# A decoder layer on one core: arrays between stages kept by chunk in DRAM, and the scan stage with another order of loads, of ACT's work, of the mask and of the keys

## The chip, the core and the metric

The kernel runs on one core of a Trainium2 chip. A core has TensorE (PE in the profile), VectorE (DVE), ScalarE (ACT), GpSimd (POOL) and SyncE (SP), each with an instruction stream of its own, and 16 DMA engines that all queues share. The metric is the device time of one execution in microseconds, the median of several.

## What is computed

One inference step of a hybrid decoder layer, all in float32: 1024 prompt tokens and 8 sample tokens of width 1024. One projection feeds two head groups, a state-space scan (SSD, 16 heads of 64, state of 128, two groups) and an mLSTM (4 heads, keys and values of 256); their outputs go through a product and a layer norm, then through PEER, a layer with product keys and gathered expert rows. Both scans go over the prompt in 8 chunks of 128 tokens. The part that matters here, per chunk:

```python
# SSD scan
acs = jnp.cumsum(dtc * a, axis=1)
lmat = jnp.exp(jnp.where(mask, acs[:, :, None] - acs[:, None], -jnp.inf))
mm = cb[..., None] * lmat * dtc[:, None]
y = jnp.einsum('btsgh,bsghp->btghp', mm, xc)
y = y + jnp.einsum('btgn,bghpn->btghp', cc, h) * jnp.exp(acs)[..., None]
h_new = h * jnp.exp(acs[:, -1])[..., None, None] + jnp.einsum('bsgn,bsgh,bsghp->bghpn', bc, decay, xc)
# mLSTM scan
att = jnp.einsum('bthd,bshd->btsh', qc, kc) * jnp.exp(dmat - m_t[:, :, None])
num = jnp.einsum('btsh,bshv->bthv', att, vc) + w_inter[..., None] * jnp.einsum('bthd,bhdv->bthv', qc, c)
c_new = w_old[..., None, None] * c + jnp.einsum('bsh,bshd,bshv->bhdv', w_s, kc, vc)
```

with `q = u_c @ w_mq` and `k = (u_c @ w_mk) * DK**-0.5`. The kernel returns the outputs of the layer and the new states of the prompt and of the eight samples.

## The kernel before

Three stages follow one another, with a barrier over all engines between them (line 107).

The **first stage** (`build`, up to line 442) makes the projection. Channels, 20 tiles of 128 (`NCT`), come out with tokens along the free dimension, go through a convolution on DVE into `cv[q]` (two buffers, q = 0, 1, line 438), through Silu on ACT (L309), and are stored by ACT's queue into `cht_d` (L311), a tile at a time: 128 rows of 1032 tokens. The rows of gates (`nacs`, `mrun`, ...) go into `rows_d`, 48 rows of 1024 tokens. DVE writes `cv[q]` again once its store has landed. What is needed by token (z, v, o) goes into `tok_d`.

The **second stage**, `build_scan`, works a chunk at a time, and beside each chunk i it updates the states of sample i. Five streams are written out by hand, one for each engine, and meet by semaphores; `pairs` runs the first two chunks written out and the other six as a loop. In a chunk i:

- SP loads `rows` (48 x 128, L600), `rb` (24 of these rows, each sent to all 128 partitions, L604), `cht` (all 20 channel tiles of the chunk's 128 tokens, L606), v (L614), and, once the mix of chunk i-1 is made (`dve_mix`), z and o (L618); then the four loads of the sample's states (`st`, `bb`, `cs`, `vb`, L623 to L626). `rb` is one buffer: its load waits until chunk i-1 has read it, and `cht` until PE's product with the state (`pe_ys`) of chunk i-1.
- PE transposes `rows`, B and x from `cht` (L660 to L668), makes q and k with channels on the partitions (L677), and then k again with tokens on the partitions (L684, `two(0)`, the source of `kw`); then the product of k and q (L690), the 16 transposes of the mix of chunk i-1 (L574), y (L700), the state's part of y (L705), the new state (L709), and the mLSTM's products up to L741, with one-column products for the sums (L718, L727, L736, and L749 for the sample).
- POOL writes `L`, the logarithms of the decays: `rb` plus a mask that is 1e30 above the diagonal (L891), 20 x 128 elements a partition. After it come `dx` (L900), `xdec` (L904), `og`, the o gate (L907), and the decay of `hT` (L909), in this order.
- ACT copies PE's transposes (`cols`, `btok`, `xtok`, L804 to L806), makes the small exponents (L809 to L816), then `root` of chunk i-1 (L566 and L568: exp(-0.5 ln) of the variances in `rs`, with a table load ahead of each of the two), then the 16 exponents of `L` (L821), the copies of q and k (L825, L826), 4 more exponents (L828), and the store of the mix of chunk i-1 (`mix_store`, L583, L586).
- DVE makes `xdt`, `kw`, `L` times C B (L948), the sums for y, the norms' statistics, the new states, and in `head_out` the variances (last L551, `dve_var`); then it waits for `root` (L553) and makes the mix (L556 to L561).

After chunk 7 ACT sends four output arrays (L859 to L862), does `root` of chunk 7, and the samples' tail follows.

The **third stage**, `build_peer`, reads `mixt_d` by chunk and quarter (L1176), and takes the rest of the time.

## Time and profile before

| | |
|---|---|
| median of 3 runs | 3868.72 us (3864.3 to 3871.62) |
| the profiled execution: its time / its span | 3861.48 us / 3859.7 us |
| first stage, span | 0 to 627.0 us |
| second stage, span | 627.0 to 1130.9 us |
| third stage, span | 1130.9 to 3859.7 us |
| busy over the span: PE, DVE, ACT, POOL | 89%, 69%, 22%, 45% |
| DMA | 1083.20 MB, mean 281 GB/s |

Times in the profile are in microseconds from the start of the span. A row of the timeline is one instruction or a run of like ones; in brackets stands how long the engine had been idle before it, and what ended that. SPq and ACTq are the queues that issue DMAs; the time of such a row is that of the issue, not of the transfer. A wait is put down to the last of its causes.

### The profile page before, as it was taken

How to read it: one execution, taken by the hardware profiler on the slowest of the kernel's cores; microseconds unless marked ns; L12 is line 12 of the kernel's file. 1: busy time of each engine (PE TensorE's matmuls, PEld its weight loads, DVE VectorE, ACT ScalarE, POOL GpSimd, SP SyncE). 2: the span in 40 equal slices, each digit the busy share in tenths (PEclk: the TensorE clock that was granted, in tenths of full speed). 3: DMA queues.
4: the chain of work that ended last, by engine and by line, in shares of the span. 5: the costliest groups of instructions: out<-in, count | busy, mean ns of one | idle time of the engine just before them, and what ended most of it. 6: DMA issues, size and time to landing. Idle time of an engine off the chain costs nothing.

```text
span 3859.7 us, 46342 instructions
## 1 busy us (share of the span) xinstructions
PE 3428.5 (89%) x15419; PEld 2392.4 (62%) x15419; DVE 2653.1 (69%) x5587; ACT 838.2 (22%) x1679; POOL 1743.5 (45%) x1432
## 2 busy tenths in 40 slices
PE   7999995988868899989997766699999999999997
PEld 6999995877743344434443443477667676667764
DVE  6660000666744789988998889777777777777776
ACT  2211111454420111121112233211111111111110
POOL 2332221222201466656765345455555555555552
PEclk9999997888879999999998989799999999999998
DMA  3333324566654799989998787999999999999996
GB/s 100 99 121 112 128 96 152 160 170 180 169 198 163 274 362 355 356 330 356 368 348 294 252 296 237 343 373 394 392 372 389 386 383 376 380 398 385 389 376 215
DMA packets 442316, 1083.20 MB, mean 281 GB/s; under 512 B 49872, under 2 KB 208048, under 8 KB 438160
## 3 DMA queue, kind: packets, MB, share of 16 engines
q0 software_dynamic: 186624, 679.56, 47.2%
q1 hardware_dynamic: 182872, 304.79, 23.3%
q10 hardware_dynamic: 72632, 96.56, 7.1%
q8 instruction: 91, 1.49, 0.2%
q14 instruction: 97, 0.79, 0.1%
HBM read 987.76 MB, written 93.02 MB: 280 GB/s over the span
## 4 chain that ended last, share of the span: by engine, by line
PE 49%; DVE 9%; DMA 8%; issue 3%; ACT 1%; POOL 1%; SPq 0%; DVEq 0%; ACTq 0%; POOLq 0%
PE PB L1921 15%; PE PB L1908 12%; PE PB L1944 8%; PE PB L1884 6%; PE PB L1866 4%; DMA x1d<-in_peer_u 3%; PE PB L1897 3%; DMA vbf<-in_peer_v,gix 3%; DVE ub L1609 2%; DVE oha L1553 1%; DMA ub<-in_peer_u,gix 1%; PE PB L1988 1%; DVE ohb L1555 1%; ACT stag L1750 1%; DVE acc L1644 1%
## 5 line engine op out<-in xcount | busy, mean ns | idle before, releaser
L1346 POOL DMA_INDIRECT ub<-in_peer_u,gix x640 | 701.7, 1096 | 855.4 <-DVE hid L1609 597.2
L1346 POOL DMA_INDIRECT vbf<-in_peer_v,gix x640 | 739.0, 1155 | 365.5 <-issue 192.8
L1921 PE MATMUL PB<-vbd,wd 128*128 128x512 f32 x1536 | 684.3, 595 | 0.0
L1944 PE MATMUL PB<-vbf,dg 128*128 128x512 f32 x1020 | 523.9, 640 | 156.1 <-ACT dg L1787 120.8
L1908 PE MATMUL PB<-xds,uts 128*128 128x384 f32 x3072 | 572.0, 341 | 0.0
L1908 PEld LDWEIGHTS PB<-xds,uts 128*128 128x128 f32 x3072 | 534.2, 190 | 0.5 <-issue 0.5
L1609 DVE CUSTOM_DVE_ANT_0 ub<-ub,x1g 128x1024 f32<-128x1024 f32 x384 | 467.7, 1223 | 77.1 <-DMA ub<-in_peer_u,gix 49.2
L1921 PEld LDWEIGHTS PB<-vbd,wd 128*128 128x128 f32 x1536 | 284.0, 191 | 308.9 <-issue 308.9
L1944 PEld LDWEIGHTS PB<-vbf,dg 128*128 128x128 f32 x1020 | 194.2, 199 | 403.9 <-issue 240.2
L1569 DVE TENSOR_TENSOR uts<-PB,uts 128x512 fp32r<-128x512 f32 x256 | 175.9, 687 | 302.2 <-ACT uts L1763 302.0
L1644 DVE SCALAR_TENSOR_TENSOR acc<-vbf,wg,acc 128x1024 f32<-128x1024 f32 x257 | 329.1, 1280 | 7.0 <-DMA vbf<-in_peer_v,gix 5.8
L1609 DVE CUSTOM_DVE_ANT_0 ub<-ub,x1gb 128x1024 f32<-128x1024 f32 x256 | 311.5, 1217 | 1.5 <-DMA ub<-in_peer_u,gix 1.3
L1763 ACT CAST uts<-PB 128x512 fp32r<-128x512 f32 x256 | 149.9, 586 | 656.1 <-PE PB L1897 644.2
L1866 PE MATMUL PB<-wo,mt 128*128 128x512 f32 x576 | 271.8, 612 | 21.5 <-DMA wo<-in_w_out 16.0
L1884 PE MATMUL PB<-wp,x1T 128*128 128x512 f32 x576 | 270.9, 604 | 2.2 <-ACT x1T L1730 2.2
L269 PE MATMUL PB<-wtkh,xh 128*128 128x256 f32 (+1 forms) x864 | 244.6, 283 | 6.2 <-ACT xps L303 6.2
L269 PE MATMUL PB<-wtkh,xl 128*128 128x256 f32 (+1 forms) x864 | 243.4, 282 | 0.0
L269 PE MATMUL PB<-wtkl,xh 128*128 128x256 f32 (+1 forms) x864 | 242.7, 281 | 0.0
L915 DVE MEMSET onec<- 128x1 f32 x1 | 0.1, 59 | 343.1 <-PEq L107 343.1
L1866 PEld LDWEIGHTS PB<-wo,mt 128*128 128x128 f32 x576 | 113.0, 197 | 167.6 <-issue 150.7
L1787 ACT ACTIVATE dg<-ident,wg 128x128 f32<-128x128 f32 x255 | 100.8, 399 | 502.2 <-PE PB L1944 424.7
L1884 PEld LDWEIGHTS PB<-wp,x1T 128*128 128x128 f32 x576 | 112.2, 196 | 144.4 <-issue 141.4
(384 smaller groups left out, 5182.1 us busy)
## 6 DMA issues: line engine op xcount, KB each, us to landing
vbd<-in_peer_v SPq DMA_DIRECT2D x128, 512.0 KB, 6.9
x1d<-in_peer_u SPq DMA_DIRECT2D x96, 512.0 KB, 9.1
gd_d<-stag ACTq DMA_DIRECT2D x12, 2048.0 KB, 10.4
gbd<-gd_d SPq DMA_DIRECT2D x16, 1536.0 KB, 18.1
ubd<-in_peer_u SPq DMA_DIRECT2D x32, 512.0 KB, 9.2
wtr<-in_w_tok SPq DMA_DIRECT2D x12, 1024.0 KB, 7.5
tok_d<-stg ACTq DMA_DIRECT2D x96, 128.0 KB, 1.7
rb<-rows_d SPq DMA_DIRECT2D x8, 1536.0 KB, 27.1
```

The source lines that it names most:

```text
L269: last = nc.tensor.matmul(PB[0:n, b, 0:TW], x[:, k, t * CH:t * CH + n], w[:, k, :], start=k == 0 and v == 0, stop=k == KD - 1 and v == 2)
L1346: pool.indirect_dma_start(out=buf, out_offset=None, in_=a[table], in_offset=bass.IndirectOffsetOnAxis(ap=index, axis=0)).then_inc(done, 16)
L1569: V.tensor_tensor(uts[:, b % 2, 1, 4 * x:4 * x + 4, :].rearrange("p k e -> p (k e)"), PB[:, 7, :], uts[:, b % 2, 0, 4 * x:4 * x + 4, :].re ...
L1609: V.tensor_tensor_reduce(out=ub[:, t % NB, :], in0=ub[:, t % NB, :], in1=by, scale=1.0, scalar=0.0, op0=ALU.mult, op1=ALU.add, accum_out=i ...
L1644: V.scalar_tensor_tensor(y, vbf[:, v % NB, :], wg[:, hv % 2, kv:kv + 1], y, ALU.mult, ALU.add).then_inc(s["ax"], 1)
L1763: S.copy(uts[:, b % 2, 0, 4 * x:4 * x + 4, :].rearrange("p k e -> p (k e)"), PB[:, 7, :]).then_inc(s["utc"], 1)
L1866: last = T.matmul(PB[:, 2 + h, :], mt[:, m % 2, j % 4, :], wo[:, j, h * 512:(h + 1) * 512], start=j == 0, stop=j == 15)
L1884: last = T.matmul(PB[:, 4 + n, :].rearrange("p (h n) -> p h n", h=4), x1T[:, kk, :], wp[:, 4 * n:4 * n + 4, kk, :], start=kk == 0, stop=kk ...
L1897: last = T.transpose(PB[:, 7, j * P:(j + 1) * P], ubd[b % 4][:, (4 * x + j) * P:(4 * x + j + 1) * P], ident[:, :])
L1908: last = T.matmul(PB[:, 6, 0:TD], uts[:, b % 2, ul, k, :], xds[:, xl, k, :], start=(k, n) == (0, 0), stop=(k, n) == (KD - 1, 2))
L1921: last = T.matmul(PB[:, 2 * d + n, :], wd[:, b % 2, d * CH:(d + 1) * CH], vbd[b % 8][:, n * 512:(n + 1) * 512], start=b == 0, stop=b == NB ...
L1944: last = T.matmul(PB[:, x, :], dg[:, n % 2, :], vbf[:, v % NB, x * 512:(x + 1) * 512], start=v % CH == 0, stop=n_pe[v + 1] == n_pe[min((c ...
```

## The change

Arrays in DRAM. `cht_d` becomes (8 chunks, 128, 20, 128) with the samples' columns in an array of their own, `chs_d`; `rows_d` becomes (8, 48, 128); `mixt_d` becomes (9, 128, 16, 128). So the loads of a chunk (`rows`, `rb`, `cht`, `mt`) and the store of the mix read and write one run for each partition; the stores of the first stage write eight pieces of 128 tokens a partition, and two DMAs count on `s_st` where one did.

The scan stage. All eight chunks are written out. SP issues the four loads of the sample's states ahead of the wait for the mix and of the loads of z and o. `root` of chunk i-1 stands ahead of ACT's copies of chunk i, and `root` of chunk 7 ahead of the output DMAs. The mask is added on DVE (`masked_rows`), for chunk n+1 between the variances of chunk n and the wait for `root`; the semaphore is `dve_l` for `pool_l`. PE makes k ahead of q, signals each (`pe_bk`, `pe_b`), and gets k by tokens from eight transposes of `kT`, which has the factor `DK ** -0.5` already. ACT copies `kT` after the fourth exponent and `qT` after the tenth.

```diff
-    cht_d = dram("cht_d", (NCT, P, NTOK))
+    cht_d = dram("cht_d", (NCH, P, NCT, CH))
+    chs_d = dram("chs_d", (P, NCT, NSMP))
-    rows_d = dram("rows_d", (NROW, SEQ))
+    rows_d = dram("rows_d", (NCH, NROW, CH))
-    mixt_d = dram("mixt_d", (16, P, NPAD))
+    mixt_d = dram("mixt_d", (NPAD // CH, P, 16, CH))
...
-                            act.dma_start(cht_d[2 * i + q, :, :], cv[q][:, :]).then_inc(s_st[q], 16)
+                            act.dma_start(cht_d[:, :, bass.ds(2 * i + q, 1), :].rearrange("c p a t -> p (c a) t"),
+                                          cv[q][:, 0:SEQ].rearrange("p (c t) -> p c t", t=CH)).then_inc(s_st[q], 16)
+                            act.dma_start(chs_d[:, bass.ds(2 * i + q, 1), :].rearrange("p a t -> p (a t)"), cv[q][:, SEQ:NTOK]).then_inc(s_st[q], 16)
...
-def pairs(eng):
-
-    for i in steps(eng, NCH // 2):
-        for q in range(2):
-            yield 2 * i + q, q
+def pairs():
+    for i in range(NCH):
+        yield i, i % 2
...
+    def masked_rows(dve, i):
+        dve.wait_ge(s["rb"], 16 * (i + 1))
+        if i == 0:
+            dve.wait_ge(s["mask"], 2)
+        free(dve, s["pe_ni"], i)
+        V.tensor_tensor(L[:, :, :], rb[:, 0:NH + MH, :],
+                        maskp[:, :].unsqueeze(1).to_broadcast([P, NH + MH, CH]), ALU.add).then_inc(s["dve_l"], 1)
...
         V.tensor_scalar(rs[0:r, 1:5], rs[0:r, 1:5], EPS, None, ALU.add).then_inc(s["dve_var"], 1)
+        if n + 1 < NCH:
+            masked_rows(dve, n + 1)
         dve.wait_ge(s["act_rs"], n + 1)
...
-        act.dma_start(mixt_d[:, :, bass.ds(lo, CH)].rearrange("j p t -> p j t"), mixT[:, :, :]).then_inc(s["stored"], 16)
+        act.dma_start(mixt_d[n], mixT[:, :, :]).then_inc(s["stored"], 16)
...
-                sp.dma_start(rb[:, :, :], rows_d[0:R_DT, bass.ds(i * CH, CH)].partition_broadcast(P)).then_inc(s["rb"], 16)
+                sp.dma_start(rb[:, :, :].rearrange("p r t -> p (r t)"), rows_d[i, 0:R_DT, :].rearrange("r t -> (r t)").partition_broadcast(P)).then_inc(s["rb"], 16)
...
-                sp.dma_start(cht[:, :, :], cht_d[:, :, bass.ds(i * CH, CH)].rearrange("j p t -> p j t")).then_inc(s["ch"], 16)
+                sp.dma_start(cht[:, :, :], cht_d[i]).then_inc(s["ch"], 16)
...
-                for w, b in ((wmq, 4), (wmk, 6)):
+                for w, b, done in ((wmk, 6, "pe_bk"), (wmq, 4, "pe_b")):
...
-                last.then_inc(s["pe_b"], 1)
-                pe.wait_ge(s["act_xt"], i + 1)
-                for h in range(MH):
-                    for k in range(KT):
-                        last = T.matmul(two(0)[:, h * DK:(h + 1) * DK], cht[:, UT0 + h * KT + k, :], wmk[:, h, k, :],
-                                        start=k == 0, stop=k == KT - 1)
+                    last.then_inc(s[done], 1)
+                pe.wait_ge(s["act_k"], i + 1)
+                pe.sem_inc(s["passed"], 1)
+                for j in range(MH * KT):
+                    last = T.transpose(two(0)[:, j * P:(j + 1) * P], kT[:, j, :], ident[:, :])
...
-                free(pool, s["pe_ni"], i)
-                G.tensor_tensor(L[:, :, :], rb[:, 0:NH + MH, :],
-                                maskp[:, :].unsqueeze(1).to_broadcast([P, NH + MH, CH]), ALU.add).then_inc(s["pool_l"], 1)
...
-                V.scalar_tensor_tensor(heads(kw[:, :], DK), heads(two(0), DK), DK ** -0.5, wide(e_ws[q][:, :], DK),
-                                       ALU.mult, ALU.mult).then_inc(s["dve_kw"], 1)
+                V.tensor_tensor(heads(kw[:, :], DK), heads(two(0), DK), wide(e_ws[q][:, :], DK), ALU.mult).then_inc(s["dve_kw"], 1)
...
-                                 mixt_d[4 * g:4 * g + 4, :, tok(ORDER[p])].rearrange("j p t -> p j t")).then_inc(s_mt[m % 2], 16)
+                                 mixt_d[ORDER[p], :, 4 * g:4 * g + 4, :]).then_inc(s_mt[m % 2], 16)
```

SP's queue around chunk 1, before; L618 are z and o, L623 to L626 the sample's states:

```order
L604 DMA rb<-rows_d 128x24x128
L606 DMA cht<-cht_d 128x20x128
L614 DMA zvo<-tok_d 128x2x512
L618 DMA zvo<-tok_d 128x2x512 x2
L623 DMA st<-in_ssd_state 128x8x128
L624 DMA bb<-bc_d 128x512
L625 DMA cs<-in_c_state 128x8x256
L626 DMA vb<-tok_d 128x2x512
```

and after, where z and o are L637:

```order
L615 DMA rb<-rows_d 128x3072
L617 DMA cht<-cht_d 128x2560
L625 DMA zvo<-tok_d 128x2x512
L629 DMA st<-in_ssd_state 128x8x128
L630 DMA bb<-bc_d 128x512
L631 DMA cs<-in_c_state 128x8x256
L632 DMA vb<-tok_d 128x2x512
L637 DMA zvo<-tok_d 128x2x512 x2
```

z and o have moved behind the four loads of the states; `rb` and `cht` have no inner runs any more.

ACT from the last small exponents of a chunk on, before:

```order
L816 ACTIVATE e_ws<-e_ws 128x4
L566 ACT_TABLE_LOAD
L566 ACTIVATE rs<-rs 128x5
L568 ACT_TABLE_LOAD
L568 ACTIVATE rs<-rs 128x5
L821 ACTIVATE L<-L,cols 128x128 x16
L825 COPY qT<-PB 128x1024
L826 ACTIVATE kT<-PB 128x1024
L828 ACTIVATE L<-L,cols 128x128 x4
```

and after, where the root, L577 and L579, stands ahead of the chunk's copies:

```order
L577 ACT_TABLE_LOAD
L577 ACTIVATE rs<-rs 128x5
L579 ACT_TABLE_LOAD
L579 ACTIVATE rs<-rs 128x5
...
L828 ACTIVATE e_ws<-e_ws 128x4
L839 ACTIVATE L<-L,cols 128x128 x4
L834 ACTIVATE kT<-PB 128x1024
L839 ACTIVATE L<-L,cols 128x128 x6
L838 COPY qT<-PB 128x1024
L839 ACTIVATE L<-L,cols 128x128 x6
L842 ACTIVATE L<-L,cols 128x128 x4
```

The root is off the way from the copies to the exponents, and `kT` comes after four of them.

DVE at the end of a chunk's `head_out`, before:

```order
L550 TENSOR_TENSOR rs<-mv,den 128x4
L551 TENSOR_SCALAR rs<-rs 128x4
L553 TENSOR_TENSOR rs<-rs,den 128x4
L556 TENSOR_SCALAR num<-num,mv,rs 128x256 x4
L559 SCALAR_TENSOR_TENSOR mix<-ysb,rs,gs 128x1024
```

and after; L545 is the mask of the next chunk:

```order
L559 TENSOR_TENSOR rs<-mv,den 128x4
L560 TENSOR_SCALAR rs<-rs 128x4
L545 TENSOR_TENSOR L<-rb,maskp 128x2560
L564 TENSOR_TENSOR rs<-rs,den 128x4
L567 TENSOR_SCALAR num<-num,mv,rs 128x256 x4
L570 SCALAR_TENSOR_TENSOR mix<-ysb,rs,gs 128x1024
```

The mask stands between the variances and the instruction that waits for the root.

## Rows read from the trace of the kernel before

**Rows 1.** By stretch: us; busy PE, PEld, DVE, ACT, POOL; PEclk, DMA share, GB/s

```profile
627.00:1130.90 503.90, 384.13 (x2372) 342.13 (x2372) 300.60 (x420) 206.16 (x539) 116.60 (x59) 0.82 0.59 163
```

**Rows 2.** Timeline, one chunk: start, us, engine line op [idle before <-releaser]

```profile
830.25 0.69 PE L663 MATMUL PB<-ident,cht 128*128 128x128 f32 x2 [6.75 <-DMA cht<-cht_d]
...
833.54 0.20 ACT L804 COPY cols<-PB 128x48 f32<-128x48 f32 x1 [9.94 <-PE PB L668]
...
835.89 1.28 ACT L566 ACT_TABLE_LOAD   x1
...
838.94 0.17 DVE L553 TENSOR_TENSOR rs<-rs,den 128x4 f32<-128x4 f32 x1 [9.43 <-ACT rs L568]
...
841.76 1.22 DVE L561 TENSOR_TENSOR mix<-num,og 128x1024 f32<-128x1024 f32 x1
...
849.51 0.62 SPq L604 DMA_DIRECT2D rb<-rows_d  x1
...
877.51 5.61 POOL L891 TENSOR_TENSOR L<-rb,maskp 128x2560 f32<-128x2560 f32 x1 [20.99 <-DMA rb<-rows_d]
...
884.50 0.69 PE L663 MATMUL PB<-ident,cht 128*128 128x128 f32 x2 [6.57 <-DMA cht<-cht_d]
```

**Rows 3.** DMA issues of the page: xcount, KB each, median us from issue to landing

```profile
rb<-rows_d SPq DMA_DIRECT2D x8, 1536.0 KB, 27.1
...
gb<-in_ln_g SPq DMA_DIRECT2D x11, 512.0 KB, 8.0
```

**Rows 4.** By stretch, as rows 1: while a load of rb runs

```profile
695.00:702.00 7.00, 7.00 (x22) 5.01 (x22) 2.10 (x2) 7.00 (x19) 0.00 (x0) 0.50 0.31 78
```

**Rows 5.** One chunk by stretch, then two of PE's lines in it

```profile
823.20:877.60 54.40, 44.12 (x281) 39.48 (x280) 36.88 (x49) 24.73 (x65) 14.07 (x8) 0.87 0.71 170
...
841.38 3.62 PE L684 MATMUL PB<-wmk,cht 128*128 128x256 f32 x16
...
847.34 1.91 PE L574 MATMUL PB<-ident,mix 128*128 128x128 f32 x16
```

**Rows 6.** Timeline of the same chunk: from the exponents to the variances

```profile
838.81 4.77 ACT L821 ACTIVATE L<-L,cols 128x128 f32<-128x128 f32 x16
...
845.29 1.27 ACT L828 ACTIVATE L<-L,cols 128x128 f32<-128x128 f32 x4
...
846.25 2.34 DVE L948 TENSOR_TENSOR L<-L,PB 128x1024 f32<-128x1024 f32 x2
...
849.08 3.68 PE L700 MATMUL PB<-xdt,L 128*128 128x64 f32 x32
...
854.62 1.90 POOL L909 TENSOR_TENSOR hT<-hT,e_hd 128x1024 f32<-128x1024 f32 x1 [3.76 <-PE PB L705]
...
860.33 1.21 DVE L972 TENSOR_TENSOR hT<-hT,PB 128x1024 f32<-128x1024 f32 x1
...
877.93 5.21 DVE L549 TENSOR_TENSOR den<-den 128x4 f32<-128x4 f32 x1
...
883.37 0.17 DVE L551 TENSOR_SCALAR rs<-rs 128x4 f32<-128x4 f32 x1
```

**Rows 7.** Timeline of chunk 0: ACT's first copy, DVE's last instruction before the root

```profile
663.71 0.20 ACT L804 COPY cols<-PB 128x48 f32<-128x48 f32 x1 [41.00 <-PE PB L668]
...
724.67 0.17 DVE L551 TENSOR_SCALAR rs<-rs 128x4 f32<-128x4 f32 x1
```

**Rows 8.** Timeline of chunk 7 and of the stage's end

```profile
1095.56 0.17 DVE L551 TENSOR_SCALAR rs<-rs 128x4 f32<-128x4 f32 x1
...
1101.36 1.28 ACT L566 ACT_TABLE_LOAD   x1 [5.92 <-issue]
...
1130.93 0.39 SPq L1176 DMA_DIRECT2D mt<-mixt_d  x1
```

**Rows 9.** First stage: a store of channels, and DVE's next write to its buffer

```profile
134.84 0.36 ACTq L311 DMA_DIRECT2D cht_d<-cv  x1
...
148.05 0.82 DVE L436 TENSOR_SCALAR cv<-xp,cw 128x1024 f32<-128x1024 f32 x1 [5.37 <-ACT xps L303]
```

More of the change, by code:

```diff
@@ L653, in _ @@
             v = zvo[:, 2:4, :].rearrange("p a n -> p (a n)")
-            for i, q in pairs(pe):
+            for i, q in pairs():
                 free(pe, s["act_nx"], i)
@@ L692, in _ @@
                 last.then_inc(s["pe_st"], 1)
-                if isinstance(i, int) and i == 0:
+                if i == 0:
                     sample_start()
@@ L798, in _ @@
             act.wait_ge(s["setup"], 1)
-            for i, q in pairs(act):
+            for i, q in pairs():
+                if i:
+                    root(act, P, i - 1)
                 act.wait_ge(s["pe_a"], i + 1)
@@ L816, in _ @@
                 S.activation(e_ws[q][:, :], e_ws[q][:, :], ACT.Exp).then_inc(s["act_small"], 1)
[L817 to L819 removed]
+                act.wait_ge(s["dve_l"], i + 1)
                 for h in range(NH):
+                    if h == 4:
+                        act.wait_ge(s["pe_bk"], i + 1)
+                        free(act, s["pe_st"], i)
+                        S.activation(kT[:, :, :].rearrange("p a n -> p (a n)"), two(6), ACT.Copy, scale=DK ** -0.5).then_inc(s["act_k"], 1)
+                    if h == 10:
+                        act.wait_ge(s["pe_b"], i + 1)
+                        free(act, s["pe_nx"], i)
+                        S.copy(qT[:, :, :].rearrange("p a n -> p (a n)"), two(4)).then_inc(s["act_qk"], 1)
                     last = S.activation(L[:, h, :], L[:, h, :], ACT.Exp, scale=-1.0, bias=cols[q][:, R_NACS + h:R_NACS + h + 1])
                 last.then_inc(s["act_l"], 1)
[L823 to L826 removed]
                 for h in range(MH):
```

70 lines of the change are left out of this document (32 added, 38 removed).

## The prediction, made before the changed kernel was run

> **What bounds the kernel now.** I read the stretches first: the scan stage runs from 627.0 to 1130.9 us, 503.9 of the 3859.7 us, and in it no engine is full: PE 384 us, DVE 301, ACT 206, DMA share 0.59 [rows 1]. The change leaves the stages ahead of it and behind it nearly alone, so the question is what paces a chunk of this stage. The reader is to see in the timeline of one chunk that it isn't an engine. Between two chunks lie 54.25 us (830.25 to 884.50, PE's first transpose of `cht`), and walked backwards they are one chain [rows 2]: PE starts a chunk when `cht` lands (884.50); `cht` stands on SP's queue behind `rb`, which landed 7.0 us earlier (877.51, POOL starts on it that moment); `rb` was issued at 849.51, 28.0 us before; SP could not issue it earlier, since it first waits for the mix of the chunk before (DVE, 841.76 + 1.22) and then sends two loads of z and o and four of the sample states, 6.5 us; and the mix waits 9.43 us for ACT's root (838.94), which ACT does only after its copies of the new chunk (833.54), that is 3.3 us after `cht` landed (830.25). Sum: 28.0 + 7.0 + 3.3 + 5.4 (copies, small exponents, two table loads, root) + 4.0 (mix) + 6.5 = 54.2. So the period is a load of 1536 KB whose wait closes a loop with the root. Eight `rb` loads take 27.1 us each in the median [rows 3]; while one ran nearly alone, the DMA queues moved 78 GB/s at a share of 0.31 [rows 4].
>
> **The stage's own sum.** It has three pieces: start to the end of chunk 0's last DVE instruction before the root (627.0 to 724.8, 97.8 us [rows 7]), seven periods up to the same instruction of chunk 7 (1095.7; 370.9 us, 53.0 each), and a tail to the next stage's first load (1130.9, 35.2 us) [rows 8].
>
> **The change part by part.**
>
> *Layout, loads.* `rb` becomes one run of 12 KB for each partition instead of 24 of 512 B, `cht` one of 10 KB instead of 20, the store of the mix 8 KB instead of 16 pieces. No row shows this `rb`; nearest are the eleven broadcasts of a 4 KB row to 128 partitions, 512 KB in 8.0 us under full load [rows 3]: three of them give 24 us as the slow end; the fast end is `cht`'s own present rate, 1280 KB in 7.0 us though cut into 2560 pieces [rows 2], 8.4 us for 1536 KB. I take 9 us, the nearer in kind, since the pieces grow in both and the broadcasts shared the queue, and 5 us for `cht`.
>
> *Order on SP.* The states' loads stand ahead of the wait for the mix, so `rb` of chunk i+1 goes out about 2 us after the mix of chunk i-1, early in chunk i, with over 25 us until DVE's mask wants it; `cht` goes out at the same event as now and has some 20 us. Both leave the loop. Put ahead of z and o: four loads of 2304 KB.
>
> *ACT.* The root stands ahead of the chunk's copies. Now it costs two table loads and two small ones from 835.89 to 838.94, 3.05 us [rows 2]. The Ln table load has no wait of its own and can run while ACT is idle; what stays behind DVE's variance is 0.2 + 1.3 + 0.2, 1.8 us (bounds 1.8 and 3.05). The copies of kT and qT move in among the exponents: the sum stays, 838.81 to 845.29, 6.5 us for 16 exponents and two copies [rows 6], but PE gets kT some 3 us earlier.
>
> *Mask.* POOL's 5.6 us go [rows 2]. On DVE I price the mask by elements: 1024 of the mix take 1.22 us, both operands in SBUF as here [rows 2], so 2560 take 3.05 us (POOL's 5.6 is the other end). It lies beside the root (1.8 us), so 1.25 us of it show on DVE, where the mix after it isn't awaited by PE for another 5 us: no cost on the path. With it goes a stall: `den`, four elements, took 5.21 us where the like of it at 883.37 took 0.17 [rows 6], because POOL's mask ran (877.51 to 883.1) [rows 2]. POOL's `dx` (1.9 us) will now meet DVE's mix; at worst 1.9 us, hidden by the same 5.
>
> *Keys.* Eight 256-column products (3.62 us) go, eight transposes come; sixteen take 1.91, so 1.0 [rows 5].
>
> *The new period, two ways.* (a) PE is busy 44.1 us in a period now [rows 5]; 44.1 - 3.6 + 1.0 = **41.5**. (b) The chain through the root: root 1.8, copies and small exponents 2.3 (833.54 to 835.89), exponents and copies 6.5, product with L 2.3 (846.25), y and its state part on PE 5.5 (849.08 to 854.62), POOL's hT 1.9, DVE from hT to its last instruction before the root 23.2 (860.33 to 883.54) less the stall 5.0 = 18.2 [rows 6]. Sum 38.5, and some 1.2 for eight handovers: **39.7**. The two are so close that PE waits little but not never; I take 42.5. The low bound is (b), 40; the high one 45, if PE keeps 3.5 us of the 10 in which it waits now. For a check I laid the present order out the same way, by the same durations and a 28 us `rb`: 53.8 a period, against 54.25 here. Of the clock the stretch of one chunk shows 0.87 granted [rows 5]; PE stands still less, so I expect no less.
>
> *Start.* ACT waits 41.0 us until chunk 0's transposes (663.71) [rows 7], of which `rb` and `cht`, at 27.1 and 7.0, are 34 us. With 9 and 5 they are 14: 20 us sooner, and 1 us back, since the weights behind them must land too. I take 19; bounds 0 and 22.
>
> *Tail.* The last root moves ahead of four output DMAs (ACT's table load at 1101.36, 5.6 us after the variance) [rows 8], but the copies behind them stay where they are, so about half, 3 us, plus 1 for the last store; bounds 2 and 6.
>
> *Stores ahead of the stage.* The 20 stores of the first stage go out as 1024 pieces of 512 B. `rb`'s price a piece, 27.1 us for 3072, gives 9.0 us; the buffer is written again 13.2 us after the store's issue (134.84 to 148.05) [rows 9]. Nothing, then; 4 us of slack a store. The loops written out I cost at nothing: in no row does an engine wait for a branch.
>
> Sum: 7 x (53.0 - 42.5) = 73.5, + 19 + 4 = 96.5 us. The profiled run took 3861.5 us, so 3765.0; its time lies 7 us under the median of the runs, 3868.7. I forecast **3766**. By the bounds (period 40 to 45, start 10 to 22, tail 2 to 6) its own range is 3742 to 3794.
>
> **Rivals.** *`rb` stays slow.* What may hold it back is the broadcast of one address to 128 partitions, not the pieces. For: `cht` has pieces of the same size and is three times as fast by the byte. Against: the 4 KB broadcasts. Then the start gains nothing (19 lost), and `rb` + `cht`, 35 us from 11 us after the variance, end PE's transposes at about 49 instead of 45: 4 us on every second chunk to every chunk, 14 to 28. Time 3799 to 3813, say 3806; 12%. The Trainium skill (DMA: Bandwidth & Descriptors, first table) counts 512 B as the least transfer for line rate; by it the cut into longer runs would bring nothing and the load would keep its time, which is this case. The trace disagrees with the rule for `rb` at least: 512 B pieces at 78 GB/s [rows 4].
>
> *A new wait: z and o late.* Their loads now stand behind four loads and beside the states' store. POOL multiplies o before it scales hT, and DVE waits for hT. It has until PE's y is done, some 18 us after the variance; they are issued at about 10. Each us over 18 costs 7 us in all; 5 over give 3801; 10%. Against it: the queue was filled from 5 us before the variance, and 2304 KB at `cht`'s present rate (1280 KB in 7.0 us) are through 12.6 us later, at about 8.
>
> *PE at the lower clock.* With transposes and one-column products the granted clock may stay half for longer, a period of 47 to 49: 3801 to 3812; 7%.
>
> *Slower.* The first stage's stores: if one took more than 13.2 us, each of 20 would hold the convolution, and PE behind it. At 20 x (x - 13.2) = 97 it eats the gain: from x = 18 us a store, twice the price above, the kernel is slower; at 20 us it takes 3861.5 - 96.5 + 136 = 3901. 2%. *Nothing moves* (the time of a chunk lies in something neither sum sees): 2%.
>
> **Numbers.** Forecast 67%, `rb` slow 12, z and o 10, clock 7, nothing 2, slower 2. The range over all but the tails: 3740 to 3813. A measurement here tells 0.2%, 8 us, from no change: faster 0.96, same 0.02, slower 0.02.
>
> **What would show it.** The period of POOL's or DVE's first instruction on `rb` at 42 to 43; `rb` to landing near 9 us and no wait for it after chunk 0; `cht` landing before PE asks; DVE's `den` at 0.2; PE busy over 95% of the middle chunks. It would be wrong if DVE's hT waited for POOL's hT behind z and o, if ACT waited on the variance with PE idle (then (b) rules and is longer than I add), or if the first stage grew from 627 us.

## The result, and the profile after it

The changed kernel takes 3750.6 us (median of 4 runs, 3749.4 to 3750.7), the kernel before 3867.6 in the same comparison (3864.3 to 3871.6). The ratio is 0.9696, 95% interval 0.968 to 0.9713: 117 us less where 3766 was forecast and 3740 to 3813 was the range. So the sign and the size held, but not by the terms of the sum: one term was missing altogether, and the three gains were all too small. That the missing cost and the missing gains nearly cancelled is luck.

By the profiled executions, cut at the same events as in the prediction:

| piece | before | forecast | after | after - before |
|---|---|---|---|---|
| first stage, to the scan stage's start | 627.1 | 627.1 | 649.7 | +22.6 |
| start, to chunk 0's variances | 97.6 | 78.6 | 72.5 | -25.1 |
| seven periods | 370.9 | 297.4 | 281.8 | -89.1 |
| tail, to the next stage's first load | 35.4 | 31.4 | 26.4 | -9.0 |
| the next stage | 2728.8 | 2728.8 | 2718.1 | -10.7 |
| span | 3859.7 | 3763.3 | 3748.5 | -111.2 |

The stretches of the profile after, first the first stage, then the scan stage (it answers to [rows 1]), then its seven periods. Columns: stretch, us, busy PE, PEld, DVE, ACT, POOL (instructions), granted clock, DMA share, GB/s.

```profile
0.00:649.70 649.70, 586.61 (x4360) 572.69 (x4360) 204.24 (x227) 124.01 (x225) 162.30 (x72) 0.97 0.34 108
649.70:1030.40 380.70, 343.44 (x2308) 311.19 (x2308) 294.09 (x428) 207.46 (x539) 78.09 (x51) 0.89 0.62 216
722.39:1003.98 281.59, 275.62 (x1904) 250.61 (x1904) 246.08 (x344) 175.23 (x456) 68.30 (x43) 0.95 0.65 223
```

The scan stage is 380.7 us where it was 503.9 [rows 1], and in its seven periods PE is now busy 275.6 of 281.6 us. The DMA issue of `rb` in the page, which answers to [rows 3]:

```profile
rb<-rows_d SPq DMA_DIRECT2D x8, 1536.0 KB, 8.4
```

8.4 us where it was 27.1 (9 was forecast). And one chunk of the timeline, from the last steps before the variances to the next ones; it answers to [rows 2, 6]:

```profile
843.49 0.17 DVE L560 TENSOR_SCALAR rs<-rs 128x4 f32<-128x4 f32 x1
843.57 2.83 DVE L545 TENSOR_TENSOR L<-rb,maskp 128x2560 f32<-128x2560 f32 x1
844.00 0.21 ACT L577 ACTIVATE rs<-rs 128x5 f32<-128x5 f32 x1
...
845.63 0.18 ACT L816 COPY cols<-PB 128x48 f32<-128x48 f32 x1
846.31 0.16 DVE L564 TENSOR_TENSOR rs<-rs,den 128x4 f32<-128x4 f32 x1
847.92 2.80 DVE L570 SCALAR_TENSOR_TENSOR mix<-ysb,rs,gs 128x1024 f32<-128x1024 f32 x1
853.47 0.35 SPq L615 DMA_DIRECT2D rb<-rows_d  x1
859.52 1.23 DVE L972 TENSOR_TENSOR t3s<-bb,cur 128x1024 f32<-128x1024 f32 x1
863.75 0.34 SPq L617 DMA_DIRECT2D cht<-cht_d  x1
...
879.00 0.47 SPq L629 DMA_DIRECT2D st<-in_ssd_state  x1
882.13 0.44 PE L674 MATMUL PB<-ident,cht 128*128 128x128 f32 x2
883.25 0.17 DVE L560 TENSOR_SCALAR rs<-rs 128x4 f32<-128x4 f32 x1
```

What the reader is to see: PE's first transpose of `cht` (882.13) has no wait for the load behind it any more, since `cht` was issued 18.4 us earlier; `rb`, issued at 853.47, isn't wanted before 883.33; the mask takes 2.83 us and lies beside the root; DVE goes on 2.8 us after the variances instead of waiting 9.43 us [rows 2]; and the next chunk's sample states are issued (879.00) before this chunk's variances (883.25). The 5.21 us stall of the four-element step [rows 6] is gone.

### The profile page after: what moved, and what is told of

Its sections match the earlier page's. It is cut to its first block, busy times and chain, and to the rows that moved or that the text cites. A ratio compares the mean times of both kernels' runs of the same rounds, so it can differ in the third digit from the quotient of the medians.

```text
span 3748.5 us, 45978 instructions
## 1 busy us (share of the span) xinstructions
PE 3372.3 (90%) x15355; PEld 2353.3 (63%) x15355; DVE 2665.5 (71%) x5595; ACT 839.6 (22%) x1679; POOL 1714.8 (46%) x1424
## 4 chain that ended last, share of the span: by engine, by line
PE 47%; DVE 12%; DMA 8%; issue 4%; ACT 1%; POOL 1%; DVEq 0%; ACTq 0%; SPq 0%; POOLq 0%
PE PB L1931 16%; PE PB L1918 13%; PE PB L1954 6%; PE PB L1894 5%; PE PB L1907 3%; DVE ub L1619 3%; DMA x1d<-in_peer_u 3%; DMA vbf<-in_peer_v,gix 3%; PE PB L1876 3%; DVE oha L1563 1%; DMA ub<-in_peer_u,gix 1%; PE PB L1998 1%; DVE acc L1654 1%; DVE ohb L1565 1%; ACT stag L1760 1%
## 5 line engine op out<-in xcount | busy, mean ns | idle before, releaser
L1356 POOL DMA_INDIRECT vbf<-in_peer_v,gix x640 | 746.9, 1167 | 357.7 <-issue 183.8
L1654 DVE SCALAR_TENSOR_TENSOR acc<-vbf,wg,acc 128x1024 f32<-128x1024 f32 x257 | 329.2, 1281 | 10.7 <-DMA vbf<-in_peer_v,gix 9.6
L270 PE MATMUL PB<-wtkh,xh 128*128 128x256 f32 (+1 forms) x864 | 244.8, 283 | 14.8 <-ACT xps L304 14.8
```

Of the source, the lines that this page charges most:

```text
L270: last = nc.tensor.matmul(PB[0:n, b, 0:TW], x[:, k, t * CH:t * CH + n], w[:, k, :], start=k == 0 and v == 0, stop=k == KD - 1 and v == 2)
L1356: pool.indirect_dma_start(out=buf, out_offset=None, in_=a[table], in_offset=bass.IndirectOffsetOnAxis(ap=index, axis=0)).then_inc(done, 16)
L1654: V.scalar_tensor_tensor(y, vbf[:, v % NB, :], wg[:, hv % 2, kv:kv + 1], y, ALU.mult, ALU.add).then_inc(s["ax"], 1)
```

## The experiments

Twelve kernels ran beside the changed one. Their times are medians of four runs (one for the last), each beside seven runs of the kernel before. The other columns come from the profiled execution of each: when the first load of `rb` is issued, from there to chunk 0's variances, the mean of the seven periods, from the last variances to the next stage's first load, and what is left of the span.

| kernel | first `rb` | start | period | tail | rest | time | ratio to before (95%) |
|---|---|---|---|---|---|---|---|
| before | 627.7 | 97.0 | 52.98 | 35.4 | 2728.8 | 3867.6 | |
| changed | 650.1 | 72.1 | 40.25 | 26.4 | 2718.1 | 3750.6 | 0.9696 (0.968-0.9713) |
| e1 channels stored whole | 627.1 | 73.2 | 40.49 | 28.3 | 2712.3 | 3730.7 | 0.9666 (0.9643-0.969) |
| e2 samples stored by SP | 643.6 | 72.1 | 40.33 | 28.8 | 2722.5 | 3742.7 | 0.9691 (0.9675-0.9707) |
| e3 `rb` in pieces | 648.3 | 89.8 | 40.99 | 27.9 | 2715.8 | 3777.3 | 0.9796 (0.9773-0.9818) |
| e4 layout alone | 645.7 | 75.8 | 50.10 | 33.9 | 2720.8 | 3829.1 | 0.9928 (0.9908-0.9948) |
| e5 root late | 648.9 | 72.3 | 41.29 | 26.5 | 2720.5 | 3761.5 | 0.9763 (0.9727-0.9798) |
| e6 mask on POOL | 651.1 | 71.1 | 40.79 | 27.9 | 2716.2 | 3757.0 | 0.9743 (0.9714-0.9772) |
| e7 keys by products | 647.8 | 71.6 | 42.25 | 27.9 | 2718.4 | 3764.3 | 0.9758 (0.9729-0.9788) |
| e8 z and o first | 648.4 | 70.3 | 44.52 | 27.9 | 2713.8 | 3779.1 | 0.9794 (0.9759-0.9829) |
| e9 order alone | 626.5 | 93.5 | 42.30 | 30.0 | 2713.2 | 3764.0 | 0.9759 (0.9734-0.9783) |
| e10 as e2, last two later | 629.3 | 69.3 | 40.22 | 28.1 | 2719.4 | 3730.6 | 0.9672 (0.9645-0.9698) |
| e11 as e1, sample loads by SP | 627.1 | 71.2 | 39.86 | 27.9 | 2725.5 | 3727.6 | 0.9664 (0.9627-0.97) |
| e12 before, once more | 627.2 | 96.4 | 52.29 | 38.9 | 2716.7 | 3847.0 | |

The medians of one kernel move by some us from comparison to comparison (the kernel before: 3867.6, 3861.5, 3858.2, 3858.4), so small effects are read from the columns, not from the times. The columns wander too. A period is 39.86 to 40.49 us in the five kernels whose loops are alike (changed, e1, e2, e10, e11) and 52.98 and 52.29 in two profiles of the kernel before, so a difference under some 0.7 us isn't resolved.

### Why the first stage grew: e1, e2, e10

The trace after shows a turn of the convolution like this (ACT, its queue and DVE):

```profile
162.44 1.07 ACT L310 ACTIVATE cv<-cv 128x1032 f32<-128x1032 f32 x1 [8.62 <-DVE cv L441]
163.67 0.43 ACTq L312 DMA_DIRECT2D cht_d<-cv  x1
164.34 0.38 ACTq L314 DMA_DIRECT2D chs_d<-cv  x1
164.84 0.73 ACT L302 COPY xp<-PB 128x688 f32<-128x688 f32 x1 [1.33 <-issue]
...
166.02 0.81 DVE L439 TENSOR_SCALAR cv<-xp,cw 128x1024 f32<-128x1024 f32 x1 [3.61 <-ACT xps L304]
...
174.44 1.07 ACT L310 ACTIVATE cv<-cv 128x1032 f32<-128x1032 f32 x1 [8.45 <-DVE cv L441]
175.67 0.39 ACTq L312 DMA_DIRECT2D cht_d<-cv  x1
176.22 0.47 ACTq L314 DMA_DIRECT2D chs_d<-cv  x1
177.22 0.73 ACT L302 COPY xp<-PB 128x688 f32<-128x688 f32 x1 [1.71 <-issue]
```

It is a closed loop: DVE convolves a tile, ACT takes its silu, issues the stores, and only then copies the next tile, on which DVE waits. ACT's copy waits for its own issues ("issue"), not for PE. From the second to the last of the 20 long stores the turns take 12.46 us each (79.68 to 304.05); in the kernel before, 11.50 (78.47 to 285.43).

e1 undoes the change of the channels' store and load:

```
-    cht_d = dram("cht_d", (NCH, P, NCT, CH))
-    chs_d = dram("chs_d", (P, NCT, NSMP))
+    cht_d = dram("cht_d", (NCT, P, NTOK))
-    act.dma_start(cht_d[:, :, bass.ds(2 * i + q, 1), :]..., cv[q][:, 0:SEQ]...)
-    act.dma_start(chs_d[:, bass.ds(2 * i + q, 1), :]..., cv[q][:, SEQ:NTOK])
+    act.dma_start(cht_d[2 * i + q, :, :], cv[q][:, :])
-    sp.dma_start(cht[:, :, :], cht_d[i])
+    sp.dma_start(cht[:, :, :], cht_d[:, :, bass.ds(i * CH, CH)].rearrange("j p t -> p j t"))
```

> The changed kernel with the convolved channels stored as before: one store of 4128 B runs for each tile, on ACT's queue, samples with it; the scan stage then reads the channels of a chunk in 512 B pieces. My theory of the 22.6 us by which the first stage grew (627.1 to 649.7): ACT and DVE form a loop there (ACT copies a tile, DVE convolves, ACT takes the silu and issues the store, ACT copies the next tile), and the second store puts about 1.06 us of issue (0.49 us from the store to the next copy before, 1.55 now) into each of 20 turns. By it the first stage ends at 627 to 631 again and the kernel takes 3728 to 3735 (3750.6 less 20, and 2 us back for the slower first load of channels). The rival, the 512 B pieces of the long store, expects the same here; a rival that lays it on something outside the stores expects 649 and 3751.

Measured: the scan stage starts at 627.1 again, 3730.7 us. The reading of the channels in 512 B pieces costs little (start 73.2 against 72.1, period 40.49 against 40.25). The same turn in e1:

```profile
168.17 1.07 ACT L309 ACTIVATE cv<-cv 128x1032 f32<-128x1032 f32 x1 [8.46 <-DVE cv L438]
169.39 0.34 ACTq L311 DMA_DIRECT2D cht_d<-cv  x1
170.26 0.73 ACT L301 COPY xp<-PB 128x688 f32<-128x688 f32 x1 [1.03 <-PE PB L245]
```

One issue, and here ACT's copy waits for PE: the loop has slack. Between 60 and 345 us that was so at 11 of e1's copies.

e2 tells the issue from the pieces. The long store keeps its eight pieces of 512 B, and only the samples' store moves to SP:

```
+    def samples_store(i, q):
+        sp.wait_ge(s_si[q], i + 1)
+        sp.dma_start(chs_d[:, bass.ds(2 * i + q, 1), :]..., cv[q][:, SEQ:NTOK])
...  (SP, behind the loads of cw and xps of tile (i, q))
+    samples_store(i - 1, q)
...  (SP, behind the loop, ahead of the next part's loads)
+    for q in range(2):
+        samples_store(NCT // 2 - 1, q)
```

> The changed kernel, with the store of the eight samples' channels (128 x 32 B a tile) issued from SP's queue instead of ACT's; the long store stays in eight pieces of 512 B a partition on ACT's queue. Theory of the issue on ACT: the first stage ends at 627 to 632, the kernel at 3727 to 3733, since ACT again issues one store of a tile. Theory of the 512 B pieces (each store lands later and holds the buffer): still 645 to 650 and 3746 to 3751. Theory of the 32 B pieces: they are still there, still 645 to 650.

Measured: 643.6 and 3742.7, between the theories and in the range of neither. The turns are back (11.25 us each, 78.45 to 280.95), so the 512 B and the 32 B pieces are not what cost. But the waits of this stretch show a new one:

```profile
POOL wtkh L378 <- DMA wtr<-in_w_tok: 27.6, 1, 27.6
...
PE PB L279 <- POOL wtkl L380: 20.6, 1, 20.6
```

The last two samples' stores wait on SP for the last silu, and the next part's weights stood behind them on SP's queue. e10 issues them behind those loads and changes nothing else.

> As the run with the samples' stores on SP's queue, but the last two of them are issued behind the loads of the next part's first weights instead of ahead of them. There POOL waited 27.6 us for those weights and PE 20.6 for POOL, and the first stage ended at 643.6, although the turns of the convolution were back at 11.3 us from 12.3. If that wait was all that ate the gain: the first stage ends at 627 to 630 and the kernel takes 3728 to 3735. If the 32 B or 512 B pieces cost something by themselves: 640 or more and 3742.

Measured: 629.3 and 3730.6 us, as the theory has it. So the 20 us are the second issue on ACT's queue inside a loop of ACT and DVE. The turns account for 17 of the 22.6 us (18 x 0.96). PE feels them at the seam to the next part, where it waits 14.8 us for ACT's last copy, 6.2 in the kernel before. The other 5 us weren't taken apart.

The Trainium skill (DMA: Bandwidth & Descriptors, "Rules for kernel authors") says that spreading DMAs over SP, ACT and GpSimd brings no bandwidth and only saves the sequencer's issue time. Of the bandwidth no run here tells. Of the issue time this case agrees, and shows what that "only" can be: e10 moves 20 stores of 4 KB from ACT to SP, and the scan stage starts 20.8 us sooner than in the changed kernel.

### Order or layout: e3, e4, e9

e3 keeps everything of the change but the layout of the rows:

```
-    rows_d = dram("rows_d", (NCH, NROW, CH))
+    rows_d = dram("rows_d", (NROW, SEQ))
-    sp.dma_start(rb[:, :, :].rearrange("p r t -> p (r t)"), rows_d[i, 0:R_DT, :]....partition_broadcast(P))
+    sp.dma_start(rb[:, :, :], rows_d[0:R_DT, bass.ds(i * CH, CH)].partition_broadcast(P))
```

> The changed kernel with the rows kept in their old layout, so that rb is again 24 pieces of 512 B for each partition, 3072 in all; order and everything else as changed. rb should land some 27 us after its issue. By my sums the order alone takes that load out of the loop: chunk 0 starts 19 us later (from 72.7 to about 92 us from the stage's start to its first variances), and of the period of 40.25 us little is lost: rb goes out about 2 us after the mix, the channels land 35 us later, and PE's transposes end 2 to 4 us late: 42 to 44 us a period, 12 to 26 us in all. Sum 3782 to 3796. If the layout were what opened the loop and the order nothing, the period would be 50 us or more and the kernel at 3840 or above.

```profile
rb<-rows_d SPq DMA_DIRECT2D x8, 1536.0 KB, 24.7
```

The load is nearly as slow as before (27.1), three times 8.4 us, and yet the period is 40.99 us, better than the 42 to 44 expected; the time, 3777.3, is 5 us under the range. The start is 17.7 us longer. So the long runs pay once, at chunk 0, and hardly in the loop: the order has taken the load out of it.

e4 is the other half: the kernel before with the new layouts of all four arrays and nothing else.

```
(before.py)
+    cht_d, chs_d, rows_d, mixt_d and their stores and loads as in the change
     order of SP's loads, root, mask on POOL, keys by products: as before
```

> The kernel before with the four arrays in the new layouts and nothing else: order of loads, root, mask on POOL and key products as before. The loop of 54.2 us loses 18.7 us of rb and 2 of the channels and is 34 us, so it no longer rules, and the next bound does: PE's 44.1 us of a period at the present clock, about 41 at a higher one, or the chain through the late root. I expect a period of 44 to 47 us (before 53.0, all changed 40.25), first variances 78 us after the stage's start, the first stage longer by 22 us: 3867.6 + 22 - 20 - 7 x 7.5 = 3817, between 3805 and 3830. So the layout would carry some 50 of the 89 us of the periods. If the order is what matters, the period stays above 50.

Measured: a period of 50.1, not 44 to 47, and so in the expectation's other case, in which the order matters. The start gained 21 us and the first stage lost 18, about as expected, and 3829.1 just fell into the range; the loop opened less than I had thought, because a second load stood in it. The timeline of one chunk:

```profile
877.74 1.22 DVE L564 TENSOR_TENSOR mix<-num,og 128x1024 f32<-128x1024 f32 x1
...
879.18 0.94 SPq L621 DMA_DIRECT2D zvo<-tok_d  x2
880.37 0.37 SPq L626 DMA_DIRECT2D st<-in_ssd_state  x1
...
882.45 3.25 SPq L629 DMA_DIRECT2D vb<-tok_d  x1
...
896.26 1.22 DVE L965 TENSOR_TENSOR t3s<-bb,cur 128x1024 f32<-128x1024 f32 x1 [11.88 <-DMA vb<-tok_d]
897.52 1.22 DVE L970 TENSOR_TENSOR ysb<-PB,dx 128x1024 f32<-128x1024 f32 x1
...
898.80 3.78 PE L717 MATMUL PB<-cst,qT 128*128 128x256 f32 x8 [6.57 <-DVE ysb L970]
```

The sample's states are issued behind the mix, the last of them lands 14 us after its issue, DVE waits 11.88 us for them, and behind DVE's `ysb` PE waits 6.57. With a fast `rb` the loop from mix to states is what is late next. In the kernel before this wait was already there behind the slow `rb`, 27.6 us of PE's idle time in seven periods (below).

e9 is the order without the layouts (e1, e3 and the mix's old layout together).

> The changed kernel with all arrays in their old layouts (channels, rows, mix), so that only the order, the mask on DVE and the keys by transposes are left of the change. First stage 627 (no second store), first variances 90 us after the stage's start and periods of 41.0, both as in the run with rb in pieces (89.8 and 40.99), tail 28 to 31, next stage 2718 to 2729: 627 + 90 + 287 + 29 + 2723 = 3756, between 3750 and 3765. If the channels' pieces, now behind a slow rb, come late to PE, up to 2 us a period more: 3770.

Measured: 42.30 a period and 3764.0, inside the range for the time; the period is 1.3 above what e3 gave, and PE waits for `cht` at four chunks, 7.8 us in all, as the last sentence allowed. The start is 93.5, not 90. The four corners together, by the period: neither 52.98, layouts alone 50.10, order and engines' moves alone 42.30, all 40.25. The order (with the mask, the root and the keys) carries 9.9 to 10.7 us of a period, the layouts 2.1 to 2.9. And by the start: 97.0, 75.8, 93.5, 72.1, that is 21 us for the layouts whatever the order.

One part of the change was never separated: the eight chunks written out. They are a loop in the kernel before and in e4 and written out in all the other variants, so what that is worth, if anything, is counted with the order here. What e5 to e8 below leave over, some 2 us a period, bounds it roughly.

### What holds the period now: e5 to e8

e5 puts the root back behind the small exponents.

```
-                if i:
-                    root(act, P, i - 1)
                 act.wait_ge(s["pe_a"], i + 1)
...
+                if i:
+                    root(act, P, i - 1)
                 act.wait_ge(s["dve_l"], i + 1)
```

> The changed kernel with ACT's root where it was before: behind the chunk's copies and small exponents. The chain that I named as the bound of a period (variance, root, copies, exponents, product with L) gets two table loads and two small ones, 3.0 us, between the small exponents and the first exponents of L, and gets back at most 0.5, since the copies wait for PE's transposes anyway. If the chain rules: 2.5 to 3 us a period, seven periods, 17 to 21 us: 3768 to 3772, period 42.8 to 43.3. If PE's work rules (76.7 us busy of 78.3 in two middle periods), PE has its query and key products meanwhile and loses only what kT comes late, 1 us or less: period 40.3 to 41.3, 3751 to 3758.

41.29 us: 1.0 of the 3.0 us of ACT's work that now lie in the chain. The waits of 800 to 1000 us (waiter, releaser, total, times, longest):

```profile
DVE rs L564 <- ACT rs L579: 18.3, 5, 3.7
...
PE PB L700 <- ACT qT L838: 7.0, 5, 1.5
```

DVE waits for the root again, 3.7 us a chunk, and PE for qT up to 1.5; the rest is hidden by PE's queries and keys. The period is that of the theory that PE's work rules (40.3 to 41.3); the time, 3761.5, lies 3.5 us over that theory's range and 6.5 under the other's.

e6 gives the mask back to POOL.

```
-    def masked_rows(dve, i):   (DVE, behind the variances)
+    def masked_rows(pool, i):  (POOL, first step of a chunk)
```

> The changed kernel with the mask on POOL again (5.6 us there, 2.83 on DVE). L comes free about 8 us before the variances, so POOL has the mask done before ACT's exponents want it; on DVE 2.8 us go from behind the variances, which PE awaits only through the mix (by the trace of the changed kernel DVE is busy 71.6 of 78.3 us in two middle periods). Against it: POOL's mask runs beside DVE's last steps before the root, where a four-element step took 5.2 us in the kernel before. Theory: POOL's mask costs DVE 2 to 5 us on the chain and gives 2.8 back off it: period 41 to 44, 3756 to 3776. If the stall is no more than what DVE saves: 40.25, 3751.

40.79: 0.5 us a period, just under the range of the theory with the stall, and less than the periods of like kernels differ. That the mask on DVE gains anything isn't shown; more than some 1 us a period it isn't.

e7 takes the keys by eight 256-column products again.

```
-                pe.wait_ge(s["act_k"], i + 1)
-                for j in range(MH * KT):
-                    last = T.transpose(two(0)[:, j * P:(j + 1) * P], kT[:, j, :], ident[:, :])
+                pe.wait_ge(s["act_xt"], i + 1)
+                for h in range(MH):
+                    for k in range(KT):
+                        last = T.matmul(two(0)[:, h * DK:(h + 1) * DK], cht[:, UT0 + h * KT + k, :], wmk[:, h, k, :], ...)
```

> The changed kernel with the keys for the state taken by eight 256-column products, 3.6 us of PE, instead of eight transposes, 1.05. If PE's work rules the period: 2.6 us more of it each, 42.8, 18 us in all and 3769. If the chain through the root rules: PE starts these products right behind its others and has them done before the scores wait for qT, so 0 to 1 us, 3751 to 3758. The granted clock may rise or fall with it; the period tells.

42.25: of 2.6 us more of PE's work 2.0 appear in the period (3764.3 where PE's theory has 3769). With e5 (1.0 of 3.0 on the chain) this is the answer to which of the two bounds is the nearer: PE's work is, and the chain through the root is so close behind it that neither can be lengthened for nothing.

e8 puts z and o, with the wait for the mix ahead of them, back in front of the sample's states.

```
                 sp.dma_start(zvo[:, 2:4, :], ...)
+                free(sp, s["dve_mix"], i)
+                for j in (0, 4):
+                    sp.dma_start(zvo[:, j:j + 2, :], ...)
                 (four loads of the sample's states)
-                free(sp, s["dve_mix"], i)
-                (z and o)
```

> The changed kernel with the loads of z and o, and the wait for the mix in front of them, ahead of the four loads of the sample's states again. With the layout alone (50.1 us a period) DVE waited 11.9 us for the last of these loads at its first step on them. Here they would be issued some 9 us after the variances instead of 4 before, and land about 13.5 us later, 22 to 23 us after the variances, where DVE and ACT want them at 16 to 17. Theory: 5 to 7 us a period, period 45 to 47.5, 3785 to 3801. Rival: the loads land in 8 us when rb isn't ahead of them, and nothing moves, 3751.

44.52, 4.3 us a period, a little under the 5 to 7 of the theory, and 3779.1, 6 us under its range. The waits of 800 to 1000 us:

```profile
DVE t3s L972 <- DMA vb<-tok_d: 22.3, 4, 9.3
ACT st L852 <- DMA vb<-tok_d: 18.9, 4, 9.0
```

It is the wait of e4 again. This one move in SP's queue is the dearest single piece of the change: 30 us of 89. Undone one by one, root, mask, keys and order of z and o add 1.0 + 0.5 + 2.0 + 4.3 = 7.8 us; all undone at once (e4 against the changed kernel) 9.9. The 2 us left over are their meeting, the written-out chunks, which e4 doesn't have, and what one profile can't resolve; these weren't told apart. The place of `rb` isn't in them, since e8 already puts the states ahead of the next `rb`, as in the kernel before.

### The start, and a version that beats both: e11

e11 is e1 with the nine sample loads at the head of the scan stage issued by SP behind its first loads instead of by ACT.

```
-            act.dma_start(chs[:, :, :], ...), rsb, nas and dts (four), ns, dsc, e_ems
                 (SP, chunk 0, behind the loads of v)
+                    sp.dma_start(chs[:, :, :], ...), rsb, nas and dts (four), ns, dsc, e_ems
```

> The kernel with whole stores of the channels (3730.7 us, first stage back at 627), and besides the nine loads for the samples at the head of the scan stage issued from SP's queue behind its own first loads instead of from ACT's. ACT spent the stretch from 649.8 to 667.8 us of the changed kernel on issuing them, one of them held it 8.9 us, while PE had chunk 0's transposes ready at 664.7: its first copy should come 3 us sooner. PE wants them some 15 us later. Expected: 3 us less, first variances 70 us after the stage's start instead of 73.2, 3725 to 3729. If they land too late on SP's queue, chunk 0 waits for them and the kernel takes 3731 or more.

In the changed kernel ACT's issues and its first copy stand like this, and PE's transposes, the last of them at 662.75 + 1.91, are ready 3.3 us before that copy:

```profile
655.42 8.87 ACTq L786 DMA_DIRECT2D dts<-rows_s_d  x1
...
662.75 1.91 PE L679 MATMUL PB<-ident,cht 128*128 128x128 f32 x8
...
667.93 0.20 ACT L816 COPY cols<-PB 128x48 f32<-128x48 f32 x1 [23.02 <-DMA e_ems<-rows_s_d]
```

In e11 ACT's first copy comes 14.4 us after the first load of `rb` (17.8 in the changed kernel). The start is 71.2 us instead of e1's 73.2, and the time 3727.6 against 3730.7. The direction is as expected; that the 3 us are a gain isn't shown, since the intervals of e1, e10 and e11 (0.9643 to 0.969, 0.9645 to 0.9698, 0.9627 to 0.97) overlap. What is shown by the columns is that any of the three, with one store a tile on ACT's queue, gives back the 20 us of the first stage: it starts the scan stage at 627.1 to 629.3, where seven kernels with two such stores start it at 645.7 to 651.1.

### The next stage: e12

> The kernel before once more, unedited, for a second profile of it. The stage behind the scan took 2728.8 us in its first profile and between 2712.3 and 2725.5 (mean 2718) in the profiles of the changed kernel and of eleven variants, among them the one with the old order and new layouts (2720.8) and the one with the mix's old layout (2713.2). If that stage is slower in the kernel before for a reason of its own, it takes 2725 to 2732 again; if the length of this stage wanders from execution to execution by itself, it takes 2712 to 2725. First stage 627 and scan stage 504 us as before, to within 2.

2716.7 us, in the middle of what all variants show (2712.3 to 2725.5). So the 2728.8 of its first profile belonged to that execution, and the 10.7 us of the table above aren't shown to be an effect of the change. e9, with the mix in its old layout, says the same (2713.2). The stage's length wanders by 16 us over these executions (2712.3 to 2728.8), and nothing smaller can be read from one of them. The first stage came out at 627.2, the scan stage at 501.3 us, a little under the 504 to within 2. The mean period repeats (52.98 and 52.29), the single ones don't: 49.5 to 56.3 us in one profile, 46.3 to 60.5 in the other.

## Why the prediction was right, and where it was not

**What bounds the kernel** (the loop from `rb` through POOL, root and mix back to `rb`): right. e3 shows it best, because there `rb` stays slow and the loop is opened by the order alone: 40.99 against 52.98. But the loop had a twin that the prediction didn't name, from the mix through the sample's states to DVE's `t3s`, hidden behind `rb`. It didn't matter for the forecast, since the same edit opened both; e4 missed by 3 to 6 us a period, with DVE waiting 64.8 us for these states and 40.4 for the root in seven periods, and e8 shows the price of the first.

**Layout, loads**: `rb` 9 forecast, 8.4 measured; `cht` 5 and 5.6. The rival in which `rb` stays slow fell: the same bytes in the same order of loads took 24.7 us in pieces of 512 B (e3) and 8.4 in runs of 12 KB. But the rival was also priced too high: 33 to 47 us on top of the forecast, where the slow load costs 27 by the medians on top of the changed kernel (e3), and 23 by start and periods. The 19 of the start are there (17.7), but not the 4 us by which `cht` was to be late on every second to every chunk: 0.7 a period.

**The stores of the first stage**: the step that failed. "Nothing, then; 4 us of slack a store" weighed when a store lands against when its buffer is written again, and that part held: the long store in pieces lands 5.1 us after its issue in the changed kernel, 3.4 in e2. The prediction itself had named a first stage that grows from 627 us as a sign of being wrong, and here it was. It left out that the change adds a second store to each tile, on ACT's queue, and that ACT stands in a loop with DVE there. Both could be read: the diff shows the second issue, and the row on which the slack was based says that DVE had waited 5.37 us for ACT's copy [rows 9]. It cost 22.6 us where 0 was forecast. The rival "slower" put its price on the right stage, but hung it on landings over 13.2 us, which never came.

**The period**: 42.5 forecast, 40.25 measured, 7 x 2.25 = 16 us more gain. The sign that it named, a period of 42 to 43, did not come. Of the two ways, (b), the chain, gave 39.7 and the trace has 39.8 between the two variances shown above. Its terms are less exact than the sum: exponents and copies take 7.9 us (847.88 to 855.76) where 6.5 stood, because ACT waits 1.0 us for PE's keys and queries, while the handovers took some 0.2 and not 1.2, and DVE's part 17.7 and not 18.2. (a), PE's work, gave 41.5 and was the mis-sized one: PE is busy 275.6 / 7 = 39.4 us in a period now. The keys did what was forecast (25.3 us of products in seven periods became 7.3 us of transposes, 2.6 each). The other 2.1 are PE's clock, and they can be seen in one line. First the kernel before, then the changed one, the queries on the state, 112 products in seven periods each; columns: busy, mean ns of one, idle before them and its releaser:

```profile
L714 PE MATMUL PB<-cst,qT 128*128 128x256 f32 x112 | 39.2, 526 | 27.6 <-DVE ysb L967 27.6
```

```profile
L724 PE MATMUL PB<-cst,qT 128*128 128x256 f32 x112 | 25.3, 379 | 0.0
```

The same instructions took 526 ns after a wait of 3.9 us a period and 379 ns without it: 39.2 - 25.3 us of busy time, 2.0 us a period. The granted clock over the periods rose from 0.88 to 0.95. In these products it shows directly. First the stretch in which they begin in a chunk of the kernel before, after PE stood still for 3.08 us, then the stretch of such a chunk's 16 in the changed kernel; the last three columns are granted clock, DMA share and GB/s:

```profile
859.30:861.90 2.60, 2.56 (x6) 2.12 (x7) 2.60 (x3) 2.60 (x7) 0.00 (x0) 0.50 0.86 123
```

```profile
865.30:868.90 3.60, 3.60 (x20) 3.19 (x18) 3.12 (x3) 3.18 (x7) 0.41 (x1) 1.00 0.77 319
```

The lower of the two levels, 1.2 GHz, behind the wait, and the full 2.4 GHz without one. The prediction had "I expect no less" of the clock and left the gain out; where this idle time of PE went, the work behind it got shorter too.

**The middle chunks**: PE over 95% busy, right (275.6 of 281.6, 98%); `den` short, right; no wait for `cht`, right. The mask 2.83 us (3.05 forecast), and the mix beside POOL's `dx` 2.80 instead of 1.28, 1.5 us where "at worst 1.9" stood. z and o did not come late: POOL waited 13.9 us for them in seven chunks (15.7 before), but its `hT` waited for PE (30.4 us), not for them, and DVE waited only 5.3 us for `hT`.

**The start**: 25 us instead of 19, beyond the bound of 22. By e4 and e9 the layouts give 21 of it and the order 4. The layouts' 21 is 2 more than the 19 that the prediction had for `rb` and `cht`; the order's 4 was not in the sum. The mask on DVE, the keys by transposes and the place of z and o are not what gives them, since e6, e7 and e8 start as early without (71.1, 71.6 and 70.3 us against 72.1). The k ahead of q and the earlier copy of kT are left, and were not measured apart.

**The tail**: 9 us instead of 4, bounds 2 and 6. Over the runs it is 26.4 to 28.8 with the change, 30.0 with the mix's old layout (e9), 35.4 and 38.9 in the kernel before. So it is 7 to 12, and the last store's layout is 1 to 4 of it.

**Rivals and the clock**: PE at the lower clock went the other way (and its 47 us a period would have given 3797, not 3801). Nothing moved, and slower by the first stage's stores: neither, though the second was nearer than its 2% said.

Errors of opposite sign, +22.6 against -16, -6 and -5, leave 4 us of error in the four pieces ahead of the next stage. The remaining 11 us, most of the distance between 3763.3 and 3748.5, are the next stage, whose length wanders by more than that from execution to execution. So 3766 came close to 3750.6 by luck in the sum, though the mechanism it stood on, the loop and its opening, was right.

## What to carry to other kernels

Before costing a new DMA at nothing, look at the engine whose queue issues it: if that engine's next instruction is awaited by an engine that it awaits itself, each issue is a term of the loop, here about 1 us a turn and 20 us in all, while the transfer is free. A load that closes a loop can be opened by order as well as by speed, and in this loop order (with the engines' moves) was worth about four times as much; but when several loads stand behind the same wait, all of them have to move ahead of it, or the next one closes the loop again. And where a change takes away idle time of TensorE, look whether its own busy time shrinks as well: here the products behind a wait of some 4 us a period began at half the clock.
